# Stick-breaking attention: scores, scaling and magnitude of the next unit issued ahead of a unit's low parts

## The reference, cut to what matters

```python
z = jnp.einsum('bhqd,bhkd->bhqk', qi.astype(jnp.float32), kf) * scale
mask = key_pos[None, :] < q_pos[:, None]
log_keep = jnp.where(mask, jax.nn.log_sigmoid(-z), 0.0)
suffix = lax.cumsum(log_keep, axis=3, reverse=True) - log_keep
a = jnp.where(mask, jnp.exp(jax.nn.log_sigmoid(z) + suffix), 0.0)
return jnp.einsum('bhqk,bhkd->bhqd', a, vf)
```

## Time and profile before

| | us |
|---|---|
| median of 3 runs | 2593.76 (2591.97 to 2595.4) |
| the profiled execution | 2593.82 |
| its span, first to last instruction | 2591.8 |
| TensorE busy | 2527.4 |
| VectorE busy | 1722.9 |
| ScalarE busy | 996.7 |
| GpSimd busy | 1292.4 |

### The profile page before, as it was taken

The page is one execution under the profiler, slowest core; times in us unless marked ns, Lnnn a source line. Parts: engine busy times, 40 slices in busy tenths (PEclk is TensorE's granted clock), DMA queues, the critical chain, the costliest instruction groups (busy, mean ns, idle before and its releaser), DMA issues.

```text
span 2591.8 us, 33360 instructions
## 1 busy us (share of the span) xinstructions
PE 2527.4 (98%) x12652; PEld 2016.9 (78%) x12652; DVE 1722.9 (66%) x2087; ACT 996.7 (38%) x1431; POOL 1292.4 (50%) x1524
## 2 busy tenths in 40 slices
PE   8999999999999999999999999989999999999997
PEld 6877887687887877877676777768878888888786
DVE  7637773768658568467766555564488777788656
ACT  3627880436315234234565545462211111111132
POOL 4632446435445445353432222224587888878653
PEclk9999999999999999999999999999999999999999
DMA  3111013222111211121310100003232233331512
GB/s 142 49 45 41 17 42 110 69 76 74 65 56 67 65 57 66 65 66 49 138 66 25 33 25 27 31 25 106 74 114 100 71 122 115 128 115 66 202 41 82
DMA packets 53527, 189.90 MB, mean 73 GB/s; under 512 B 5440, under 2 KB 5824, under 8 KB 53376
## 3 DMA queue, kind: packets, MB, share of 16 engines
q1 hardware_dynamic: 31392, 110.11, 12.8%
q10 hardware_dynamic: 21984, 77.73, 8.3%
HBM read 158.33 MB, written 29.49 MB: 72 GB/s over the span
## 4 chain that ended last, share of the span: by engine, by line
PE 83%; DVE 10%; ACT 4%; issue 2%; POOL 0%; ACTq 0%; DVEq 0%; POOLq 0%
PE PS L903 39%; PE PS L1675 10%; PE PS L1649 5%; PE PS L1633 5%; PE PS L1254 4%; PE PS L1160 2%; PE PS L1050 2%; PE PS L1697 2%; PE PS L1081 1%; PE PS L1487 1%; PE PS L1470 1%; PE PS L1066 1%; PE PS L1510 1%; PE PS L1601 1%; PE PS L1287 1%
## 5 line engine op out<-in xcount | busy, mean ns | idle before, releaser
L706 POOL CAST w_hi<-w_stage 128x1024 fp32r<-128x1024 f32 x122 | 148.2, 1215 | 843.4 <-PE PS L903 698.2
L709 POOL TENSOR_TENSOR w_lo<-w_stage,w_hi 128x256 fp32r<-128x256 f32 x488 | 467.9, 989 | 9.8
L903 PE MATMUL PS<-XH,w_hi 128*128 128x512 f32 x1216 | 383.7, 397 | 5.9 <-DVE XL L2815 1.8
L903 PE MATMUL PS<-XL,w_hi 128*128 128x512 f32 x1216 | 375.3, 390 | 0.0
L903 PE MATMUL PS<-XH,w_lo 128*128 128x512 f32 x1216 | 375.1, 390 | 0.0
L903 PEld LDWEIGHTS PS<-XH,w_hi 128*128 128x128 f32 x1216 | 223.2, 188 | 56.9 <-issue 9.0
L903 PEld LDWEIGHTS PS<-XL,w_hi 128*128 128x128 f32 x1216 | 228.2, 188 | 48.7
L903 PEld LDWEIGHTS PS<-XH,w_lo 128*128 128x128 f32 x1216 | 228.2, 188 | 48.4
L806 POOL TENSOR_TENSOR w_lo<-w_stage,w_hi 128x256 fp32r<-128x256 f32 x246 | 207.3, 848 | 0.0
L802 POOL CAST w_hi<-w_stage 128x256 fp32r<-128x256 f32 x246 | 133.2, 545 | 112.8 <-PE PS L903 38.8
L1675 PE MATMUL PS<-ffn_u_hi,w_hi 128*128 128x512 f32 x392 | 152.8, 390 | 2.3 <-DVE H L3358 2.2
(11 more groups left out here) (500 smaller groups left out, 6103.3 us busy)
## 6 DMA issues: line engine op xcount, KB each, us to landing
w_stage<-w SPq DMA_DIRECT2D x202, 512.0 KB, 3.3
H<-h_kept ACTq DMA_DIRECT2D x20, 1024.0 KB, 4.9
ssd_sum_rows<-sums_kept ACTq DMA_DIRECT2D x32, 512.0 KB, 3.5
h_kept<-H ACTq DMA_DIRECT2D x16, 1024.0 KB, 5.0
H<-x_t ACTq DMA_DIRECT2D x8, 512.0 KB, 8.3
pj_kept<-ple_proj_tiles ACTq DMA_DIRECT2D x8, 512.0 KB, 2.6
h_kept<-H ACTq DMA_DIRECT2D x8, 512.0 KB, 3.0
out_t<-out_tiles SPq DMA_DIRECT2D x16, 256.0 KB, 2.1
```

Of the source, the lines that this page charges most:

```text
L706: nc.gpsimd.tensor_copy(w_hi[:, slot, :, :], w_stage[:, slot, :, :]).then_inc(s_w_hi, 1)
L709: nc.gpsimd.tensor_tensor(w_lo[:, slot, k:k + 2, :], w_stage[:, slot, k:k + 2, :], w_hi[:, slot, k:k + 2, :].bitcast(F32), ALU.subtract).t ...
L903: mm = nc.tensor.matmul(outs[:, half, :], wt[:, slot, k, :], a[:, k - first, half * HB:(half + 1) * HB], start=(k == whole[0] and wt is w_ ...
```

## The change

In every step, K of the unit that follows is issued ahead of S instead of behind the late pieces. Scaling of the unit that follows comes directly behind d in DVE's order, ahead of the taps and the unit's own maximum and low part. The magnitude of the unit that follows comes directly behind the unit's high copy on ScalarE. A pair's units 0 and 1 are issued in step 0, K(1) behind the late pieces as before. TensorE's order in step s is then: early pieces, K(s+1), S(s-1), V(s-2), H, late pieces, C(s-1). What scaling waits for is the same: the scores of its unit, and the values of the unit three before.

```diff
--- before.py
+++ after.py
@@ -1546,12 +1546,11 @@
             for m in range(4):
                 for step in range(SB_STEPS):
                     early, late = SB_FILL[m][step]
-                    if step == 0:
-                        sb_pieces(early)
+                    sb_pieces(early)
                     if step == 0:
                         sb_scores(m, 0)
-                    else:
-                        sb_pieces(early)
+                    elif step + 1 < NU:
+                        sb_scores(m, step + 1)
                     if 1 <= step <= NU:
                         sb_suffix(m, step - 1)
                     if step >= 2:
@@ -1563,8 +1562,8 @@
                     sb_pieces(late)
                     if m == 3 and step == NU:
                         out2_tiles(0, range(0, 2))
-                    if step + 1 < NU:
-                        sb_scores(m, step + 1)
+                    if step == 0:
+                        sb_scores(m, 1)
                     if 1 <= step <= NU:
                         sb_carry(m, step - 1)
             assert progress[0] == 8 * len(SB_ORDER)
@@ -2306,13 +2305,18 @@
             inverse_root(RM[:, :], flat(1), D, EPS6, mix["v"].sem, mix["v"].base, mix["rs"].sem)
             sb_copies(SB_ORDER[2])
             nc.scalar.preload_act_table_set("natural_log_exp_and_others")
+            def sb_magnitude(m, t):
+                q0, T = SB_WIDE[t], NU * m + t
+                act.wait_ge(s_zc, T + 1)
+                nc.scalar.activation(SPF[:, T % 3, :, q0:HB], ZS[:, T % 3, :, q0:HB], ACT.Abs).then_inc(s_al, 1)
+
             for m in range(4):
                 for step in range(SB_STEPS):
+                    if step == 0:
+                        sb_magnitude(m, 0)
                     if step < NU:
                         q0, T = SB_WIDE[step], NU * m + step
-                        z, l = ZS[:, T % 3, :, q0:HB], SPF[:, T % 3, :, q0:HB]
-                        act.wait_ge(s_zc, T + 1)
-                        nc.scalar.activation(l, z, ACT.Abs).then_inc(s_al, 1)
+                        l = SPF[:, T % 3, :, q0:HB]
                     for key in sb_finished(m, step, 0):
                         sb_copies(key)
                     if (m, step + 1) in HEAD_STEPS and step == 1:
@@ -2337,6 +2341,8 @@
                     if step < NU:
                         act.wait_ge(s_sp, T + 1)
                         nc.scalar.activation(SPH[:, T % 3, :, q0:HB], l, ACT.Copy).then_inc(s_sph, 1)
+                    if step + 1 < NU:
+                        sb_magnitude(m, step + 1)
                     if (m, step) in HEAD_STEPS:
                         head_root(HEAD_STEPS[m, step])
                     if step == NU and m == 3:
@@ -3148,18 +3154,22 @@
             sb_lows(("k", 0))
             v_scaled(0)
             root_squared()
+            def sb_scaled(m, t):
+                (hf, j), q0, T = SB_UNITS[t], SB_WIDE[t], NU * m + t
+                dve.wait_ge(s_z, T + 1)
+                if T >= 3:
+                    dve.wait_ge(s_o, T - 2)
+                v.scalar_tensor_tensor(out=ZS[:, T % 3, :, q0:HB], in0=PS[:, 0:2, q0:HB], scalar=RK[:, j:j + 1],
+                                       in1=RM[:, hf * HB + q0:(hf + 1) * HB].unsqueeze(1).to_broadcast([P, 2, HB - q0]),
+                                       op0=ALU.mult, op1=ALU.mult).then_inc(s_zc, 1)
+
             for m in range(4):
                 for step in range(SB_STEPS):
+                    if step == 0:
+                        sb_scaled(m, 0)
                     if step < NU:
                         q0, T = SB_WIDE[step], NU * m + step
                         z = ZS[:, T % 3, :, q0:HB]
-                        dve.wait_ge(s_z, T + 1)
-                        if T >= 3:
-                            dve.wait_ge(s_o, T - 2)
-                        hf, j = SB_UNITS[step]
-                        v.scalar_tensor_tensor(out=z, in0=PS[:, 0:2, q0:HB], scalar=RK[:, j:j + 1],
-                                               in1=RM[:, hf * HB + q0:(hf + 1) * HB].unsqueeze(1).to_broadcast([P, 2, HB - q0]),
-                                               op0=ALU.mult, op1=ALU.mult).then_inc(s_zc, 1)
                     if step == 6:
                         attended(m, 0)
                     if m == 3 and step == NU:
@@ -3173,6 +3183,8 @@
                         d_ = ZS[:, T1 % 3, :, q1:HB]
                         dve.wait_ge(s_su, T1 + 1)
                         v.tensor_tensor(d_, d_, PS[:, 2:4, q1:HB], ALU.subtract).then_inc(s_d, 1)
+                    if step + 1 < NU:
+                        sb_scaled(m, step + 1)
                     if m == 3 and step == NU:
                         v.memset(SM[:, 8, 0:1], 0.0).then_inc(s_evac[1], 13)
                         head_lo(0)
```

## The result

The changed kernel takes 2612.51 us (median of 4 runs, 2610.82 to 2613.85) against 2594.03 us before (also 4 runs): slower by 18.5 us, ratio 1.0074 with a 95% interval of 1.0061 to 1.0086. The forecast was 2606.2 us, 12.4 us slower, with a range of 2599 to 2614.

A forecast was written before the change was run, and what follows sets the result against it. The prediction took PE, busy 98% of the span, as the bound. Head pairs 1 and 2 at +3.8 us each, pair 3 at +3.6 and pair 0 at +1.2 gave +12.4 us on 2593.82: 2606.2 us, range 2599 to 2614.

The forecast's parts named there:

- C waits for d: In the attention stage the carry would wait for VectorE's difference, 0.4 to 0.5 us per wide step, bounds 0 and 0.9.
- P behind the head sums: In step 5 of three head pairs the weight piece's bank wait loses its cover by the scores: +0.9 us each.
- P behind the cu product: In step 7 of pairs 1 and 2 the weight piece waits for a bank freed only after scaling: +2.1 us each.
- The ring: VectorE's chain from suffix product to suffix product: 7.2 us instead of 8.1 without a tap, 8.3 with one.
- Scaling under POOL: On VectorE beside POOL, scaling stays at 1.28 us; by the other reading the sum is about 1.2 us higher.
- rival C: Added TensorE waits of 1 to 3.3 us drop its clock: +4 to +7 us, 2612 us; chance 0.17.
- The slack of pair 0's last steps: In pair 0, wide steps 8 to 11 return about half of what is added, 1.8 us, an estimate.
- Rival A: In the attention stage banks come free sooner, leaving only carry waits and switching, 4.5 us: 2598.3 us; chance 0.10.
- Rival B: Shorter softplus chain removes all 10.3 us of suffix-product waits, less about 2 us of carry waits: 2585.5 us; chance 0.05.

The follow-up runs named there:

- e2_lows_first: The changed kernel with the next unit's scaling on VectorE moved behind taps and bank-freeing products, directly ahead of the maximum: 2605.45 us, ratio 1.0044 to the kernel before.
- e4_gap_pe_after: The changed kernel with the next unit's scaling on VectorE moved between a unit's maximum and its low part: 2599.84 us, ratio 1.0025 to the kernel before.

## Why the prediction was right in its direction and short in its size

*C waits for d* (0.4 to 0.5 us a step, "a dozen places"): held; 4.5 us in 12 waits (0.3 to 0.5 us each), in every run with TensorE's changed order. In the others it is 0.9 to 1.2 us in 3 or 4.

*P behind the head sums* (+0.9 each in step 5): held; S(4) to S(5) of pair 1 is 10.13 us against 9.10. In step 2 there is such a wait too (0.83 us idle, 3.28 us from H to P), so there are six and not three. I had put step 2 at +0.3 because H no longer waits for L3101. That wait did go, and S(1) to S(2) of pair 1 is 9.17 against 9.12; over S(0) to S(4) the pair is 0.41 us longer. The K that now stands ahead of S makes S(0) of each pair 0.9 us later, and S(10), which has no K ahead of it any more, gives that back. Pairs 1 and 2 came within 0.25 us of their forecast.

*P behind the cu product* (+2.1): held, 9.58 less 7.33 is 2.25. The run with the bank products first takes 1.16 of it away. In step 8 of pair 3 the prediction has P 4.85 us after S; its own terms (1.23, 1.14, 1.20, 1.22, 0.14) add up to 4.93, and 4.93 was measured.

*The ring*: its form held. In pair 3, S(9) to S(10) was put at 8.3 and measured 8.51; S(7) to S(8) 8.6 and 8.76. In the ring, it is from the tap to the maximum that takes longer than put: 1.31 us instead of 1.1 to 1.2.

*Scaling under POOL*: none of the 48 scalings took over 1.29 us in the changed kernel or in any other of the profiled ones, and in the changed kernel ten of those over 1024 columns ran beside POOL's L709 (the one at 1490.85, shown above, is one). A low part in pair 0 of the changed kernel, with two inputs in SBUF, took 1.66 us beside L709:

```profile
1390.66 1.66 DVE L3205 TENSOR_TENSOR sb_softplus_lo<-sb_softplus,sb_softplus_hi 128x1024 fp32r<-128x1024 f32 x1 [1.12 <-ACT sb_softplus_hi L2343]
```

The Trainium skill ("VectorE: DVE Perf Modes", section "Two Vector instructions with no wait between them") has an operation with two SBUF tensor inputs read the second one through an interface shared with GpSimd; scaling has one such input only. The trace agrees. Two such inputs do not always cost time, though: a maximum at 1415.66 in the same trace took its ordinary 1.22 us beside L709.

*The step that was mis-sized is the clock*. I had set it apart as rival C with a chance of 0.17, instead of putting it into the sum; it put the clock at +4 to +7 us and the time at 2612 us. Measured were 2612.51 us, with 4.1 us of clock by the count below, and the range held because it reached over this rival. The table by stage for the same three stretches (S(5) to S(6) and S(8) to S(9) of pair 0, S(10) to S(11) of pair 3; the third number from the end is the granted clock), in the changed kernel:

```profile
1364.73:1375.92 11.19, 8.36 (x39) 6.21 (x39) 4.83 (x5) 5.37 (x6) 2.98 (x5) 0.85 0.15 48
1392.37:1403.57 11.20, 11.20 (x55) 8.39 (x55) 7.28 (x6) 6.38 (x8) 1.93 (x3) 0.85 0.15 48
1749.39:1758.72 9.33, 8.87 (x37) 6.44 (x37) 6.01 (x6) 4.27 (x5) 0.39 (x1) 0.67 0.00 0
```

and in the run with the scaling in the gap and the same TensorE order:

```profile
1364.99:1373.38 8.39, 6.75 (x39) 4.98 (x38) 5.18 (x5) 5.50 (x6) 2.98 (x5) 1.00 0.19 64
1388.92:1398.53 9.61, 9.61 (x54) 7.18 (x54) 7.20 (x6) 6.34 (x8) 2.63 (x4) 1.00 0.15 56
1739.64:1748.09 8.45, 7.63 (x36) 5.67 (x37) 6.01 (x6) 4.88 (x5) 0.74 (x1) 0.80 0.00 0
```

In the first two, about the same number of products take 1.6 us longer each in PE's busy time (8.36 less 6.75, 11.20 less 9.61), and a clock of 0.85 over 11.2 us is 1.7 us lost. They follow a 2.83 us wait for the cu product and a 2.19 us wait of S(8); in the other run these two waits are 1.64 and 0.98 us. In the third, the changed kernel takes 0.88 us longer than the other run (9.33 against 8.45), which itself has one slow stretch there (0.80), where the changed kernel has more (0.67). That is 4.1 us together; 12.4 and 4.1 make 16.5 of the 17.4 us by which S(11) of pair 3 is later. The other 0.9 us are spread over all pairs: with the clock taken out, pair 0 is 1.5 us longer against a forecast of 1.2, pairs 1 and 2 are 4.05 and 4.02 against 3.8, and pair 3 is 3.8 against 3.6. The slack of pair 0's last steps had been put at 1.8 us as an estimate: from S(8) to S(11), the clock aside, 2.3 us came back.

*Rival A* (banks free sooner than read, 2598.3 us) fell by the rows of steps 5 and 7. *Rival B* (faster) fell for the reason given against it. But it named something real: with scaling out of the way of the banks and K left as a cover, the shorter chain is worth the 5.2 us of the run with the scaling in the gap and TensorE's old order.

What stays open: S(11) of pair 3 is 17.4 us later, the profiled span is 17.0 us longer, and the medians are 18.5 us apart. The profiled execution of the changed kernel is the fastest of its four (2610.82 us), that of the kernel before is 0.2 us below its median; no run here says why the others of the changed kernel took 1.5 to 3 us more.

## What to carry to other kernels

A block of work that looks movable because its own inputs are early may be standing where it stands as a cover for others' waits: before moving it, look at which instruction behind it starts at the same small distance (here 0.14 us) after another engine is done with a buffer, without any idle time shown. An operation issued early on an in-order engine is better put into that engine's own idle gap (here the 1.1 us between maximum and low part) than ahead of the instructions that free a buffer. And where waits are added on TensorE, put the slow products that may follow them into the sum, not only into the rivals.

## What the runs showed of the hardware that was not expected

Waits of much the same length had different sequels. Behind S(10)'s 3.39 us the clock was 0.67 of full speed over the 9.33 us that follow in the changed kernel, and S itself began slow. In the run with the bank products first (e2_lows_first) the same S waited 3.41 us and began at full speed, and the clock was 0.80 over the 8.44 us that follow:

```profile
1744.32 0.73 PE L1487 MATMUL PS<-sb_softplus_hi,from_r 128*128 128x512 f32 x2 [3.41 <-DVE sb_softplus_lo L3205]
```

In the kernel before, a 2.31 us wait at the same place left the clock at full speed (S's first two products 0.72 us), and a 2.24 us wait one step later did not the earlier trace rows:

```profile
1741.28 1.22 PE L1487 MATMUL PS<-sb_softplus_hi,from_r 128*128 128x512 f32 x2 [2.24 <-DVE sb_softplus_lo L3193]
```

The drop is between the two levels, 1.2 and 2.4 GHz: behind the 3.39 us wait S's second pair of products starts 1.02 us after the first, where one step earlier in the same trace it starts 0.57 us after. The run with the bank products first had the same two drops in pair 0 as the changed kernel; the wait ahead of the first was 1.64 us instead of 2.83, that of S(8) 2.19 us in both:

```profile
1363.77:1373.73 9.96, 8.32 (x39) 6.21 (x38) 4.84 (x5) 5.38 (x6) 2.98 (x5) 0.83 0.16 54
1390.11:1401.25 11.14, 11.14 (x54) 8.22 (x55) 7.19 (x6) 6.35 (x8) 1.93 (x3) 0.85 0.14 49
```

The run with the scaling in the gap and the same TensorE order (e4_gap_pe_after) has the same 1.64 us wait at the first place, and its clock stays at 1.00. So the length of the wait alone doesn't say whether the clock falls. About 3 of the 5.6 us between these two runs (9.96 less 8.39 and 11.14 less 9.61) are the clock, and not the ring.
